# One transformer layer on one core: a token-routed expert block whose last tables, first weights and a gelu move across the border between its two halves

## The reference

```python
def apply_block(args):
    hk, ek, gk = args                    # tokens, chosen experts (8 heads x 16), gates
    u = u_table[ek]
    act = jax.nn.gelu(jnp.einsum('btd,btrkd->btrk', hk, u).astype(jnp.float32))
    w = (gk * act).astype(hk.dtype)
    return jnp.einsum('btrk,btrkd->btd', w, v_table[ek])
```

## Time and profile before

| what | value |
|---|---|
| median of 3 runs (lowest to highest) | 3967.8 us (3966.8 to 3970.59) |
| the profiled execution | 3965.28 us |
| its span | 3963.5 us |
| mean granted TensorE clock | 0.974 |
| PE, DVE, ACT, POOL busy | 3700.7, 2861.7, 1140.4, 2312.2 us |
| dense up-projection, last block ends | 2888.0 us into the span |
| dense down-projection, PE's first matmul | 2983.9 us |

### The profile page before, as it was taken

One profiled execution on the slowest core, in us unless ns is written; L12 is line 12 of the kernel. 1 busy time (PEld: TensorE's weight loads), 2 busy tenths in 40 slices (PEclk: granted clock), 3 DMA queues, 4 the chain that ended last, 5 costly groups with the idle time before them and its releaser, 6 DMA issues. The chain is left out here.

```text
span 3963.5 us, 49639 instructions
## 1 busy us (share of the span) xinstructions
PE 3700.7 (93%) x17969; PEld 3211.3 (81%) x17969; DVE 2861.7 (72%) x3863; ACT 1140.4 (29%) x1377; POOL 2312.2 (58%) x1290
## 2 busy tenths in 40 slices
PE   6999999999988999999999999999918999999998
PEld 5778888787767688879999999999817888888886
DVE  7666666667762445869778656666658999999998
ACT  3232322333211332223333222222202333333332
POOL 7334343344433234446666648888877888887870
PEclk9999999999999999999999999999959999999999
DMA  6888888887877586998998889999878999999994
GB/s 230 279 292 279 291 284 283 288 294 275 296 260 255 185 296 226 387 397 279 351 313 276 276 286 341 339 342 339 330 282 345 388 373 382 383 382 373 386 374 188
DMA packets 409612, 1231.15 MB, mean 311 GB/s; under 512 B 77561, under 2 KB 122633, under 8 KB 327977
## 3 DMA queue, kind: packets, MB, share of 16 engines
q1 hardware_dynamic: 261784, 770.07, 55.9%
q0 software_dynamic: 63488, 302.31, 20.2%
q10 hardware_dynamic: 84240, 157.63, 10.8%
HBM read 1020.65 MB, written 344.45 MB: 344 GB/s over the span
## 5 line engine op out<-in xcount | busy, mean ns | idle before, releaser
L767 POOL TENSOR_TENSOR wlo<-raw,whi 128x1024 fp32r<-128x1024 f32 x296 | 758.8, 2586 | 1075.2 <-ACT whi L1122 527.7
L1315 PE MATMUL bank<-h_hi,whi 128*128 128x384 f32 (+1 forms) x3312 | 1191.9, 360 | 41.6 <-DVE wlo L1642 37.2
L1317 PE MATMUL bank<-h_hi,wlo 128*128 128x384 f32 (+1 forms) x3312 | 1181.3, 357 | 0.0
L1316 PE MATMUL bank<-h_lo,whi 128*128 128x384 f32 (+1 forms) x3312 | 1180.5, 356 | 0.0
L1315 PEld LDWEIGHTS bank<-h_hi,whi 128*128 128x128 f32 x3312 | 625.4, 189 | 99.9 <-DVE wlo L1642 45.4
L1317 PEld LDWEIGHTS bank<-h_hi,wlo 128*128 128x128 f32 x3312 | 624.9, 189 | 50.2
L1316 PEld LDWEIGHTS bank<-h_lo,whi 128*128 128x128 f32 x3312 | 625.6, 189 | 47.9 <-issue 0.2
L1642 DVE TENSOR_TENSOR wlo<-raw,whi 128x2048 fp32r<-128x2048 f32 x240 | 549.3, 2289 | 142.0 <-ACT whi L1241 84.6
L1613 PE MATMUL bank<-whi,ew_hi 128*128 128x512 f32 x1408 | 550.1, 391 | 98.1 <-DVE ew_lo L1642 95.9
L834 POOL DMA_INDIRECT gates_d<-gate_all,place_u x336 | 496.0, 1476 | 148.3 <-issue 129.8
L1615 PE MATMUL bank<-whi,ew_lo 128*128 128x512 f32 x1408 | 548.8, 390 | 0.0
(11 more groups left out here) (302 smaller groups left out, 4713.4 us busy)
## 6 DMA issues: line engine op xcount, KB each, us to landing
raw<-in_weights SPq DMA_DIRECT2D x388, 1024.0 KB
v_rows_d<-in_weights ACTq DMA_DIRECT2D x96, 1024.0 KB
tin<-in_weights SPq DMA_DIRECT2D x162, 512.0 KB, 6.0
u_rows_d<-tout SPq DMA_DIRECT2D x324, 256.0 KB, 6.8
u_rows_d<-u_tout SPq DMA_DIRECT2D x188, 256.0 KB
v_rows_d<-in_weights SPq DMA_DIRECT2D x32, 1024.0 KB
gates_d<-zeros SPq DMA_DIRECT2D x32, 768.0 KB, 16.1
act_d<-act_o ACTq DMA_DIRECT2D x128, 192.0 KB
```

Of the source, the lines that this page charges most:

```text
L767: pool.tensor_tensor(wlo[slot][:, part], raw[slot][:, part], whi[slot][:, part].bitcast(F32), ALU.subtract).then_inc(lo_made, 1)
L1315: pe.matmul(bank, whi[slot][:, cols], rhs_hi(c), start=c == 0, stop=False)
L1316: pe.matmul(bank, whi[slot][:, cols], rhs_lo(c), start=False, stop=False)
L1317: last = pe.matmul(bank, wlo[slot][:, cols], rhs_hi(c), start=False, stop=c == DC - 1)
```

## The change

Four things move; no arithmetic is added or left out.

1. `scatters_before(k)` is 200 + 2k in place of 200 + 1.5k, so two scatters stand behind each gather, and all 384 are issued ahead of gather 92 (before: ahead of gather 123).
2. SP issues `load_aux(0, q)`, with its wait for all scatters, right behind the load of up slab 122 (`AUX_FROM`), ahead of the loads of 123 to 127.
3. DVE makes the first weights in slabs 124 to 127, one quarter in each, and `wlo` of down slab 0 ahead of picks 107 to 127, not behind them.
4. The gelu of `act_p` on ACT comes behind the second `whi` copy of pair 0, and the multiplication with the gates comes right ahead of the first `add_row`.

```diff
+AUX_FROM = N_U - 6
 def scatters_before(k):
-    return min(TD * PICKS, FIRST_SCATTERS + (3 * k + 1) // 2)
+    return min(TD * PICKS, FIRST_SCATTERS + 2 * k)
...
             for e in range(U_POOL + 2, N_U + 1):
                 load_unit(e, raw_landed[e % 2])
                 if e - 2 in TURN_U:
                     store_rows(u_tout[e % 2], e - 2, tab_stored[e % 2])
+                if e == AUX_FROM:
+                    for t in range(TD):
+                        sp.wait_ge(gate_placed[t], 16 * PICKS)
+                    for h in range(2):
+                        sp.wait_ge(act_stored[h], 16 * 8 + 16)
+                    for q in range(4):
+                        load_aux(0, q)
...
             expert_slab(1, raw_landed[1])
-            for t in range(TD):
-                sp.wait_ge(gate_placed[t], 16 * PICKS)
-            for h in range(2):
-                sp.wait_ge(act_stored[h], 16 * 8 + 16)
-            for q in range(4):
-                load_aux(0, q)
...
-            act.wait_ge(u_used, PICKS)
-            act.activation(act_p[:, :], act_p[:, :], ACT.Gelu_apprx_tanh).then_inc(acts_made, 1)
...
+                    if J == 0 and m == 1:
+                        act.wait_ge(u_used, PICKS)
+                        act.activation(act_p[:, :], act_p[:, :], ACT.Gelu_apprx_tanh).then_inc(acts_made, 1)
...
                 while dots < PICKS and dot_slab(dots) <= e:
                     dot(dots)
                     dots += 1
+                if e >= N_U - 4:
+                    first_weights(e - N_U + 4)
+            dve.drain()
+            low_part(0, 0)
             for k in range(dots, PICKS):
                 dot(k)
-            dve.drain()
-            low_part(0, 0)
-            for q in range(4):
-                first_weights(q)
-            dve.wait_ge(acts_made, 1)
-            tt(act_p[:, :], act_p[:, :], gate_p, ALU.mult)
...
                 if k == 0:
+                    dve.wait_ge(acts_made, 1)
+                    tt(act_p[:, :], act_p[:, :], gate_p, ALU.mult)
```

More of the change, by code:

```diff
@@ L627, in _, with load_aux @@
                                      h_td_d.rearrange("p (c b i) -> p b c i", c=DC, b=4)[:, b]).then_inc(h_tok_landed, 16)
+            def load_aux(J, q):
+                sbn, at = 2 * J + q // 2, pair_of(q)
+                sp.dma_start(act_in[q // 2][:, at, :], act_d[bass.ds(sbn, 1), :, at, :].rearrange("a p b t -> (a p) b t")
+                             ).then_inc(aux_landed[q], 16)
+                sp.dma_start(gate_in[q // 2][:, at, :], gates_d[bass.ds(sbn, 1), :, at, :].rearrange("a p b t -> (a p) b t")
+                             ).then_inc(aux_landed[q], 16)
             def load_unit(e, landed):
@@ L2219, in add_row @@
                     return
+                if k == 0:
+                    dve.wait_ge(acts_made, 1)
+                    tt(act_p[:, :], act_p[:, :], gate_p, ALU.mult)
                 dve.drain()
```

## The result

The changed kernel is slower, and by more than was predicted: 4024.7 us (median of 4 runs, 4016.9 to 4026.5) against 3967.3 us before (4 runs); after over before is 1.014, 95% interval 1.0122 to 1.0157. Forecast: 3980, range 3957 to 4000. The profiled execution has a span of 4021.7 us (before 3963.5), 58.2 us more, where the sum had +12.3.

The account below looks back on a forecast made before the run. POOL's count of issues, not the transfers, was taken to set the rows' pace. The terms +6.9 +2.4 +3 = +12.3 us on 3965.3 gave 3977.6, and the runs' median, 2.5 above, 3980; range 3957 to 4000.

Parts of the forecast that it names:

- Part 1: Between gathers 3 and 92: 45 more scatters at 1.27 us each delay gather 92 by 57 us.
- The ledger: POOL from 2334 to 2880: 1.27 us per issue plus 1.28 us per dot or `wlo` make up the time.
- dear scatters: Rival, moved scatters: each costs 1.96 us, held by each other's completion; +88 there, sum +43, 4011 us; chance 0.05.
- Part 2: Up slabs 120 to 127: gathers come alone, PE sets the pace at 8.3 us a slab; slab 127 ends at 2938.
- The early loads: Slabs 120 to 127: eight loads, 3.1 MB, beside gathers and slab loads cost 5 us, bounds 0 to 9.
- Part 3: The tail, dots 107 to 127: 3.0 us a row from dot 110 on, bounds 2.6 and 3.5; ends at 2999.
- Part 4: The border: down slab 0 runs under the dots, the slow start moves to slab 1, +2.4 us; slab 2 at +9.3.
- Part 5: Behind the last dot: POOL's `v` rows come late for a PE further ahead; 3 us, bounds 0 to 8.
- gather 92 near 2854: Sign in the profile after: gather 92 starts near 2854 if the scatter price holds, near 2815 if it is wrong.
- slabs 120 to 127 in 67 to 75 us: Sign in the profile after: the last eight up slabs take 67 to 75 us.
- the last dot near 2999: Sign at the end of the tail: last dot near 2999; the prediction falls if it ends below 2990.
- the gap behind down slab 0: Sign on PE at the border: a hole of 45 to 60 us behind down slab 0, not ahead of it.

Follow-up runs that it names:

- e1: The kernel before with two scatters per gather in place of one and a half, all else unchanged; 4013.7 us, 1.0131 over before.
- e5: The kernel before with 16 more scatters ahead of the first gather and 14 more behind gather 2; 3953.2 us, 0.997 over before.
- e12: The changed kernel with every scatter behind the first 200 cut to 96 of its 128 tokens; 3987.0 us, 1.0059 over before.
- e3: The changed kernel with every scatter behind the first 200 cut to 64 of its 128 tokens; 3981.9 us, 1.0046 over before.
- e11: The changed kernel with the four first weights put back behind the tail's dots; 4025.4 us, 1.0153 over before.
- e13: The changed kernel with two row buffers in use in place of three from gather 109 on; 4040.2 us, 1.0188 over before.

## Why the prediction was wrong

The sign, the places and the border were right, the sum was not. By its own parts, on the span:

- **Part 1, the price of a moved scatter: this step failed.** 45 x 1.27 = +57 was put, +83.7 measured, 1.86 us each. The ledger had POOL's issues and DVE's holds and no term for the window. It gave back the kernel before to 0.1 us, but that was no test: the 1.28 us of a DVE operation had been taken from 2334 to 2880, the stretch that holds gathers 3 to 92, and so had swallowed the 6.7 us of the 8 held issues there. At two scatters per gather three of the five transfers that may be under way are scatters, and the next waits for a row that takes 8.1 us from issue to dot (mean of gathers 4 to 91). Error: 27 us. The rival "dear scatters" (1.96 each, +88, chance 0.05) named this size and nearly its cause, "held by each other's completion"; its 1660 ns mean was no evidence for it, and I set it aside with that.
- **Part 2, slabs 120 to 127.** PE's pace came out: eight slabs in 66.6 us in e1. But dots 92 to 107 took 64.9 us there, not the 71 worked out without loads (76 with them): dot 107 follows `wlo` 127 and starts 7 us ahead of PE's end of slab 127 (2950.3 and 2957.2), while the prediction put both at 2938. The early loads, put at 5 us (0 to 9), cost 17.8 (e1 against the changed kernel). The hole on PE, from a queue in which a slab load stands behind 3.1 MB, was not in the sum. The two errors partly cancel; for the stretch 7 us are left.
- **Part 3, the tail.** 3.0 us a row was taken, 3.65 measured for the last 17. The upper bound of 3.5 was passed too. The bounds came from bytes (2.6) and from dots 124 to 126 before (3.5), the value between from POOL's hold; no term was made for a row's way of 6.9 us over three buffers. Error: 15 us.
- **Part 4, the border.** Slab 0 ran early and the slow start moved to slab 1 as said. The changed kernel's first 8.3 us of slab 1 had a clock of 0.77 (1.2 GHz for part of them), the next 1.00:

```profile
3045.80:3054.10 8.30, 8.27 (x29) 6.72 (x30) 5.20 (x5) 2.93 (x4) 6.47 (x7) 0.77 0.85 313
3054.10:3062.40 8.30, 8.30 (x38) 6.90 (x37) 4.14 (x4) 2.83 (x3) 3.27 (x3) 1.00 0.54 182
```

  Counted from the last dot, slab 2 starts 14.0 us earlier than before (13.4 predicted). This part was right.
- **Part 5, the `v` rows.** 14.0 us at slab 2 are 8.8 at the end, so 5.2 were given back (3 put, 0 to 8). Beside the earlier trace rows's 2.2 us the changed kernel's waits of DVE from 2976 to 3120 have

```profile
DVE res L2228 <- DMA row<-v_rows_d,expert_u: 6.1, 1, 6.1
DVE res L2243 <- DMA part<-in_weights,part_u: 1.3, 1, 1.3
```

The errors add up: -4.5 (gather 3 earlier; gather 0 lies between 2289.5 and 2304.3 over all profiles here, whatever the kernel) + 27 + 7 + 15 + 2, some 46, between +12 and +58. Of "what would show it", gather 92 near 2854 failed (2875.7), so did slabs 120 to 127 in 67 to 75 us (82), and so did the last dot near 2999 (3041.0); the gap behind down slab 0, 69 us, is long because the tail is.

## What to carry to other kernels

A ledger that gives back the schedule from which its terms were taken proves nothing, and terms taken where a limit hardly bites don't hold where it bites often: before it prices a denser mix of transfers, look for the few issues that were idle for more than the usual gap, and count what was under way at each. Work that only has to be early belongs where its engine stands idle (e5: 30 scatters in POOL's two gaps of 23 us, 0.3% of the kernel), not where it moves its neighbours. And a load put ahead on a shared queue delays what stands behind it: count the bytes ahead of the next slab, not only their total.

## What the runs showed of the hardware that I had not expected

- POOL's indirect transfers are bounded in elements under way. Here an issue that would have made 768 was held (39 times in the changed kernel, 12 in e12, once in e3), and 640 or 704 passed; with one and a half scatters per gather 768 passed at times. The profile marks the wait as `issue` with no releaser.
- An indirect issue of 64 elements takes 0.90 us and one of 96 takes 0.91, against 0.97 for 128: nearly all of it does not depend on the count.
- A gather's 1 MB takes 6.9 us from the end of the issue to the dot with three rows under way and 2.7 MB of other loads in the 62 us (changed kernel), 5.6 to 5.9 with three and at most 1.4 MB (e1, e5, e11), and 4.9 with two (e13).
